# Order of sums, loads and streamed products at the turn from attention to a Strassen-like FFN

## What is computed

```python
h = rmsnorm(x, norm1_gain) * (1.0 + scale1) + shift1
proj = h @ w_in                                   # q | k | v | p
...
x = x + gate1 * (merged @ w_out)
h2 = rmsnorm(x, norm2_gain) * (1.0 + scale2) + shift2
ffn = (silu(h2 @ w_gate) * (h2 @ w_up)) @ w_down
x = x + gate2 * ffn
```

## Time and profile before

| | us |
|---|---|
| median of 3 runs | 1036.49 |
| their lowest and highest | 1035.93, 1039.36 |
| the profiled execution | 1040.24 |
| its span, first to last instruction | 1038.5 |

### The profile page before, as it was taken

How to read it: one execution, slowest core, us unless ns; L and a number is a source line. 1 busy time by engine, 2 the same in 40 slices (tenths; PEclk the granted TensorE clock), 3 DMA queues, 4 the chain that set the end, 5 groups by cost and what they waited for, 6 DMA issues and landing times.

```text
span 1038.5 us, 13419 instructions
## 1 busy us (share of the span) xinstructions
PE 981.9 (95%) x4656; PEld 821.4 (79%) x4656; DVE 695.4 (67%) x1089; ACT 380.8 (37%) x722; POOL 213.2 (21%) x167
## 2 busy tenths in 40 slices
PE   6989999989988798999999999999999999999998
PEld 6878888877876676878788787887878788787876
DVE  4777887885688595765756566565656666665554
ACT  1756667575343453142231413223141322304120
POOL 2032233344221003122220112222011222202220
PEclk9999999999999898999999999999999999999999
DMA  9963333445134365445233543533454253345223
GB/s 363 364 235 132 126 134 120 153 159 192 52 122 142 102 215 210 162 144 213 90 137 145 202 162 121 206 117 122 162 203 162 95 195 130 146 162 201 81 81 162
DMA packets 83669, 166.69 MB, mean 161 GB/s; under 512 B 5312, under 2 KB 52144, under 8 KB 83632
## 3 DMA queue, kind: packets, MB, share of 16 engines
q1 hardware_dynamic: 78400, 155.28, 42.3%
q10 hardware_dynamic: 5232, 10.95, 2.9%
HBM read 151.13 MB, written 15.07 MB: 160 GB/s over the span
## 4 chain that ended last, share of the span: by engine, by line
PE 70%; DMA 11%; DVE 9%; ACT 3%; SPq 3%; issue 2%; POOL 1%; ACTq 1%; DVEq 0%
PE ps L1581 22%; PE ps L1582 22%; PE ps L1583 22%; DMA bs<-bs_scratch 7%; DMA wi_raw<-in_w_in 2%; SPq L416 1%; DVE x L1197 1%; DMA bs_scratch<-stg 1%; DVE wo_raw L1177 1%; PE ps L1692 1%; PE ps L1794 1%; DVE g_acc L1119 1%; SPq L418 1%; DVE xn L1354 1%; DMA sinks<-in_attn_sinks 1%
## 5 line engine op out<-in xcount | busy, mean ns | idle before, releaser
L1437 DVE TENSOR_TENSOR x<-x,ps 128x512 f32<-128x512 f32 x176 | 120.8, 687 | 83.6 <-PE ps L1583 82.8
L1581 PE MATMUL ps<-h_hi,ring 128*128 128x512 f32 x352 | 137.6, 391 | 0.0
L1582 PE MATMUL ps<-h_lo,ring 128*128 128x512 f32 x352 | 137.2, 390 | 0.0
L1583 PE MATMUL ps<-h_hi,ring 128*128 128x512 f32 x352 | 137.2, 390 | 0.0
L1581 PE MATMUL ps<-wd_hi,act_hi 128*128 128x512 f32 x352 | 136.9, 389 | 0.0
L1582 PE MATMUL ps<-wd_lo,act_hi 128*128 128x512 f32 x352 | 136.9, 389 | 0.0
L1583 PE MATMUL ps<-wd_hi,act_lo 128*128 128x512 f32 x352 | 136.9, 389 | 0.0
L1581 PE MATMUL ps<-bs,ring 128*128 128x512 f32 x264 | 105.0, 398 | 15.4 <-DMA bs<-bs_scratch 15.4
L1043 POOL TENSOR_TENSOR wd_lo<-raw_d,wd_hi 128x1024 fp32r<-128x1024 f32 x22 | 57.4, 2628 | 301.0 <-ACT wd_hi L813 301.0
L1393 DVE TENSOR_TENSOR ring<-s,ring 128x512 fp32r<-128x512 f32 x88 | 73.8, 841 | 60.6 <-ACT ring L782 60.4
L1038 POOL TENSOR_TENSOR raw_d<-raw_d,g2bc 128x1024 f32<-128x1024 f32 x22 | 57.3, 2625 | 234.6 <-DMA raw_d<-in_w_down 234.6
(11 more groups left out here) (215 smaller groups left out, 1795.8 us busy)
## 6 DMA issues: line engine op xcount, KB each, us to landing
bs<-bs_scratch SPq DMA_DIRECT2D x126, 512.0 KB, 6.0
stage<-in_w_ada SPq DMA_DIRECT2D x24, 512.0 KB, 5.5
raw_g<-in_w_gate SPq DMA_DIRECT2D x11, 1024.0 KB, 5.1
raw_u<-in_w_up SPq DMA_DIRECT2D x11, 1024.0 KB, 7.1
raw_d<-in_w_down SPq DMA_DIRECT2D x11, 1024.0 KB, 8.9
wi_raw<-in_w_in SPq DMA_DIRECT2D x8, 640.0 KB, 18.8
x_st<-in_x ACTq DMA_DIRECT2D x8, 512.0 KB, 5.3
ada_in_raw<-in_w_ada SPq DMA_DIRECT2D x8, 512.0 KB, 8.5
```

What stands on the lines that cost most here:

```text
L1437: dve.tensor_tensor(xt, xt, bank(DB[j % 4]), ALU.add).then_inc(down_evac, 1)
L1581: pe.matmul(dst, s_hi, m_hi, start=start, stop=False, skip_group_check=onto)
L1582: pe.matmul(dst, s_hi, m_lo, start=False, stop=False, skip_group_check=onto)
L1583: return pe.matmul(dst, s_lo, m_hi, start=False, stop=stop, skip_group_check=onto)
```

## The change

1. The loads of g1bc and g2bc (512 KB each) go from ACT's list at tile 1 to SP's list ahead of the first stage loads.
2. At tile 0 ACT evicts kT before pext.
3. `m_low` of tiles 3 to 7 goes from POOL to DVE.
4. Around tile 7 of stage 2, DVE makes the operands A11 and A12 ahead of the last `t_low` of tile 4, and the sums `a_sum13`, `a_sum2` of pair 0 at other places; ACT's order follows.
5. For tiles 6 and 7 the order of T3, T2, T4, T1, B22 is turned (B22 ahead of T1, T3 behind T2); tile 7's first sum has its own half of g1bc; ACT's wait for `t_back` goes.
6. On SP, the loads of pair 1's raw weights go behind the stores of B22 and the stream load for S4.
7. In every pair A22 is one product (`streamed_products`): gate and up take turns by k.

```diff
-            (6, T3), (6, T2), (7, T2), (7, T3), (6, T4), (7, T4), (6, T1), (7, T1), (6, B22), (7, B22)]
+            (6, T2), (7, T2), (6, T3), (7, T3), (6, T4), (7, T4), (6, B22), (7, B22), (6, T1), (7, T1)]
...
+        def tmp3(t):
+            return g1bc[:, HALF:] if t == 7 else g1bc[:, 0:HALF]
...
-            load_raw(1, 0)
-            load_raw(1, 1)
             store_stage(6, B22)
             store_stage(7, B22)
             sp.wait_ge(t_out, 32 * 4)
             sp.wait_ge(stg_out[0], 32 * 4)
             sp.wait_ge(stg_out[1], 32 * 4)
             load_stream(0, 2, first=True)
+            load_raw(1, 0)
+            load_raw(1, 1)
...
+                    if a == 0:
+                        evac_k(a)
                     act.wait_ge(pT_done, a + 1)
...
-            act.wait_ge(t_back, 16 * 3)
-            t_high(6, T3)
             copy_p1(0, 0, first=True)
...
-                if t + 3 < NT:
-                    m_low(t + 3)
...
             mixed_sum(0, 1)
+            dve.wait_ge(mlo_done, 3)
+            m_low(3)
...
+                    if t == NT - 3:
+                        a_low(0, A11, 0, 0)
+                        a_low(0, A11, 1, 0)
+                        a_low(0, A12, 0, 0)
+                        a_low(0, A12, 1, 0)
+                    t_low(t - 1, B22)
...
+            def streamed_products(p, o, par, dst, n, direct=None):
+
+                for m in range(2):
+                    pe.wait_ge(a_lo, prod(p, o, m))
+                if not direct:
+                    pe.wait_ge(bs_in, 64 * (3 * p + n - 1))
+                for k in range(KT // 2):
+                    b_hi, b_lo = (bs2[0][:, k, :], bs2[1][:, k, :]) if direct == T4 else (bs[:, k, 0, :], bs[:, k, 1, :])
+                    for m in range(2):
+                        r = ring[m][(par + o) % 2]
+                        last = mm3(bank(dst[m]), r[:, 0, k, :], r[:, 1, k, :], b_hi, b_lo, False, k == KT // 2 - 1, True)
+                        if k == KT // 2 - 1:
+                            last.then_inc(prod_done, 1)
+                        elif m == 1 and direct != T4:
+                            last.then_inc(bs_used, 1)
...
-                for m in range(2):
-                    pe.wait_ge(taken, 10 * p + 3 + m)
-                    stream_product(p, A22, m, par, GB, False, 1, T4 if first else None)
+                pe.wait_ge(taken, 10 * p + 4)
+                streamed_products(p, A22, par, GB, 1, T4 if first else None)
```

More of the change, by code:

```diff
@@ L657, in exps, with evac_k @@
                 act.activation(sinkex[:, ch, :], sinkin[:, ch, :], ACT.Exp).then_inc(exp_done, 1)
+            def evac_k(a):
+                act.wait_ge(kT_done, a + 1)
+                kps = bank(6)[:, 0:2 * P].rearrange("p (k c q) -> p k c q", k=NKV, c=2)
+                for ch in range(2):
+                    last = act.activation(kT[:, :, a % 2 + 2 * ch, :], kps[:, :, ch, :], ACT.Copy,
+                                          scale=vcol[:, KG:KG + 1])
+                last.then_inc(kT_evac, 1)
             def evac_ssm(t):
@@ L721, in _ @@
                     evac_o(z, 0)
[L722 to L728, removed]
+                if 1 <= a < NT:
+                    evac_k(a)
                 if it == NT:
@@ L886, in _ @@
             h2_rows_act(7)
+            a_high(0, S2, 1, 0, first=True)
             t_high(6, T2)
-            a_high(0, S2, 1, 0, first=True)
             t_high(7, T2)
+            t_high(6, T3)
             t_high(7, T3)
@@ L897, in _ @@
             a_high(0, A22, 1, 0, first=True)
+            t_high(6, B22)
+            t_high(7, B22)
             t_high(6, T1)
             t_high(7, T1)
-            t_high(6, B22)
-            t_high(7, B22)
             a_high(0, S1, 0, 0, first=True)
@@ L1437, in add_down, with m_low @@
                 dve.tensor_tensor(xt, xt, bank(DB[j % 4]), ALU.add).then_inc(down_evac, 1)
+            def m_low(t):
+                dve.wait_ge(mhi_done, t + 1)
+                dve.tensor_tensor(h_lo[:, :, tok(t)], m_raw[:, :, tok(t)], h_hi[:, :, tok(t)].bitcast(F32),
+                                  ALU.subtract).then_inc(mlo_done, 1)
             mixed_sum(0, 1)
-            for t in range(1, NT):
-                if t + 1 < NT:
-                    mixed_sum(t + 1, 0)
-                if t == NT - 2:
[L1444 to L1448, removed]
-                    a_sum13(0, 0, first=True)
[L1450 to L1467, removed]
@@ new lines, in _ @@
+            dve.wait_ge(mlo_done, 3)
+            m_low(3)
+            for t in range(1, NT - 1):
+                mixed_sum(t + 1, 0)
+                mixed_sum(t, 1)
+                h2_rows(t - 1)
+                if t == NT - 2:
+                    a_sum13(0, 0, first=True)
+                if t - 1 in HALF0:
+                    h2_low(t - 1)
+                    if t + 3 < NT:
+                        m_low(t + 3)
+                else:
+                    t_sums(t - 1)
+                    t_sum4(t - 1)
+                    if t + 3 < NT:
+                        m_low(t + 3)
+                    t_low(t - 1, T3)
+                    t_low(t - 1, T4)
+                    t_low(t - 1, T2)
+                    t_low(t - 1, T1)
+                    if t == NT - 3:
[4 more added lines that the diff above has]
+                    t_low(t - 1, B22)
+                for k in FOLD2.get(t, ()):
+                    fold_gate2(k)
@@ L1468, in _ @@
+            a_sum13(0, 1, first=True)
+            mixed_sum(7, 1)
+            h2_rows(6)
+            a_sum2(0, 0, first=True)
             a_sum2(0, 1, first=True)
-            h2_rows(6)
             t_sums(6)
             t_sum4(6)
-            t_low(6, T3)
             a_low(0, S2, 0, 0)
@@ L1475, in _ @@
             t_sums(7)
+            a_low(0, S2, 1, 0)
             t_low(6, T2)
-            a_low(0, S2, 1, 0)
             t_low(7, T2)
+            t_low(6, T3)
             t_low(7, T3)
@@ L1490, in _ @@
             a_low(0, A22, 1, 0)
+            t_low(6, B22)
+            t_low(7, B22)
             a_sum4(0, 0)
             a_sum4(0, 1)
+            take_sum(u3s, p1s, 0, GB, 0, S3)
             t_low(6, T1)
             t_low(7, T1)
-            take_sum(u3s, p1s, 0, GB, 0, S3)
-            t_low(6, B22)
-            t_low(7, B22)
             take_sum(u3s, p1s, 1, GB, 0, S3)
@@ L1858, in stream_product @@
                 for k in range(KT // 2):
[L1859 to L1862, removed]
+                    last = mm3(bank(dst[m]), r[:, 0, k, :], r[:, 1, k, :], bs[:, k, 0, :], bs[:, k, 1, :],
+                               False, k == KT // 2 - 1, True)
+                    if m == 1 and k < KT // 2 - 1:
                         last.then_inc(bs_used, 1)
@@ L1896, in products_b @@
                     pe.wait_ge(taken, 10 * p + 1 + m)
-                    stream_product(p, S3, m, par, GB, False, 0, T3 if first else None)
+                    stream_product(p, S3, m, par, GB, 0, T3 if first else None)
             def products_c(p, par, first=False):
```

17 lines of the change are left out of this document (8 added, 9 removed).

## The result

The changed kernel takes 1020.69 us (median of 4 runs, 1019.79 to 1021.35) where the kernel before took 1037.92 us in the same measurement (4 runs, 1035.93 to 1040.7): a ratio of 0.983, 95% interval 0.980 to 0.986. It is faster, by 17.2 us or 1.7%. The forecast was 27.2 us of gain, 1009.3 us with a range of 1000 to 1020: too much by 10 us, and the time lies 0.7 us above the range. The profiled execution took 1021.35 us with a span of 1019.6 us, 18.9 us less than the span of before.

What follows compares the result with a forecast made beforehand. PE, busy 981.9 us, was taken as the bound, so only its idle time and slow stretches could be won: 12.6 (term 1) + 13.0 (terms 2 to 5) + 1.6 (term 6) = 27.2, giving 1009.3 us, range 1000 to 1020.

Steps and rivals of the forecast that it cites:

- Term 1: In every pair, A22 by k removes PE's wait for bs ahead of S4: 12.6 us over ten pairs.
- Term 2: Low rests of tiles 3 to 7 from POOL to DVE: DVE reaches tile 7's first sum 2.4 us earlier.
- Term 3: Around tile 7, operands out of PE's way: with Term 2, the awaited x sum ends at 330.9, 7.0 us earlier.
- Term 4: The turn of tiles 6 and 7: B22 is ready at 358.4 us, 19.0 us earlier.
- term 6: The start, at tile 0: issues and pext off the chain, 1.6 us less, bounds -1.0 and +3.3.
- Term 5: Stores and loads between B22 and pair 0's S4: 6.0 us given back, S4 at 380.5, stall some 8 us.
- A: Before pair 0's S4, raw weights do not hold it: S4 starts at 372, time 1001; chance 0.12.
- C: In the pairs, the last slot still lands behind S1: Term 1 gives 0, time 1022; chance 0.07.
- D: In the pairs, coupled halves delay S4's operand: slower than before, 1044 at 3.5 us wait per pair; chance 0.02.
- E: In the pairs, alternating banks costs clock: 2.6 us in each of ten, 1035, no change; chance 0.04.
- B: The turn gives little: terms 2 to 5 give 4 us instead of 13, time 1018; chance 0.12.

Runs made afterwards that it cites:

- the two kernels alone: A22 by k as the only change to the kernel before: 1025.34 us; A22 as two products again on the changed kernel: 1033.56 us.
- mlow_pool: Changed kernel with the low rests of tiles 3 to 7 made by POOL again: 1023.56 us.
- tback: Changed kernel with ACT's wait for the three loads back (t_back) again ahead of pair 0's first copy: 1025.70 us.
- no_turn: Changed kernel with T1 of tiles 6 and 7 made ahead of B22 again, on ACT and DVE: 1025.83 us.
- take_first: Changed kernel with DVE's take of S1's first bank, in pair 0 alone, right behind the takes of A22: 1016.04 us.
- gate2_late: Changed kernel with take_gate2, DVE's copy of the second gate row, moved behind DVE's second half of pair 0: 1023.16 us.
- raws_first: Changed kernel with SP's raw loads of pair 1's gate and up weights ahead of B22's stores again: 1010.99 us.
- sums_late: Changed kernel with DVE's sums of pair 1's weights moved behind the second half of pair 0: 1014.22 us.

## Why the predicted time was too low, step by step

- **Term 1** was right: 12.6 forecast, 12.4 and 12.9 measured by the two kernels alone. In the profiled executions the stretch from S4's end in pair 0 to the end is 11.2 us shorter (636.97 to 625.82): the period came out at 60.06 and not 59.9 us, for the first matmul of S4, which was to lose the 0.27 us above its share, still takes 0.49 us though it waits for nothing.
- **Terms 2 and 3** were right as a position. The second x sum of tile 6 ended at 329.61 us where 330.9 less the start's 1.6 was forecast, and PE's longest wait for x fell from 4.8 to 1.0 us. Term 2 undone costs 2.9 us (mlow_pool), where 2.4 was forecast. Term 3, the place of the eight instructions, was not undone by itself; what it gives in time is not shown.
- **Term 4** was right as a position: the last low rest of B22 ended at 357.26 us (forecast 358.4, 356.8 with term 6). Two parts of it undone, ACT's wait (tback) and the last step of the turn (no_turn), cost 5.0 and 5.1 us. DVE:

```profile
355.97 1.29 DVE L1391 TENSOR_TENSOR stg<-xn,stg 128x512 fp32r<-128x512 f32 x2
```

- **Term 5 is the step that failed**, and within it the sentence "2 sums, 2 of `take_gate2`, a take and a low rest, 6 x 0.6 = 3.8. S4 starts at 380.5". Its transfers were right: the streams went out at 362.36 (363.4 forecast) and raw_u was in at 375.9 (376.7); PE was ready at 372.1 (372). From there S4 took 10.9 us and not 3.8 (6 x 0.6 is 3.6; the sum has a slip of 0.2). I followed S4's operand and forgot its bank: behind the operand DVE does five more instructions and then, as the sixth, the take that frees the bank, some 3.6 us at 0.6 each (take_first: 4.7 us less with that take alone moved). And I set every DVE instruction at 0.6 us, though `take_gate2` sets POOL's scaling free, which then held two others, the low rest of S4's operand and the gate's product behind it, for 3.2 us together (gate2_late: S4 4.4 us sooner without the scaling and the 1.2 us of the copy). So the stall was 14.7 us in place of 8, S4 started 7.9 us later than the forecast with its start term, and with the 1.4 us by which the pairs gave less than term 1 and an S4 that ran 1.0 us shorter, this is the 8.3 us between 27.2 and the 18.9 of the profiled executions.
- The price that the prediction gave to the moved raw loads was too low with it. It put the time that is given back between B22's last low rest and S4 at 6.0 us; that stretch went from 16.1 us (377.39 to 393.46) to 29.5 (357.26 to 386.78), 13.4 us more, and raws_first shows 9.7 us for the moved loads with what hangs on them. A margin on S4's start would have held the result: the range had bounds for rivals that moved the time down to 1000, and none for a later gate.
- **Term 6** cannot be told from none in time; the wait that it was to shorten did shorten, from 2.2 to 0.5 us.

The undone edits together are 12.9 + 2.9 + 5.0 + 5.1 + 1.1 = 27.0 us, and the raw loads' move takes 9.7 back: 17.3, where 17.2 was measured. That match is luck in part: each number has an error of some 3 us, and term 3 and the rest of the turn are not among them. It doesn't rule out a further cause of a few us. What is shown is the stall: sums_late took it away, and take_first, raws_first and gate2_late moved its parts one by one.

Of the rivals, A had the right place and the wrong sign: the raw loads did not land before DVE wanted them. C and D are excluded by term 1's kernels and by the pairs' period, E by the clock of 1.00 in the pairs. B needs a closer look. Its amount came nearly true: all edits but term 1 give some 4.5 us and not 13.0 + 1.6, and its 1018 lies nearer to 1020.7 than 1009.3 does. Its causes did not: the turn's last step carries over (no_turn), and PE has no wait for the read-back of T3 left. The gain was lost behind the turn, at S4.

The Trainium skill, in "DMA: Bandwidth & Descriptors", section "Anatomy of one DMA — SWDGE (gpsimd) path", gives its formula for a single transfer issued from GpSimd, while these were six issued from SP. By the estimate worked out from it, the 4 MB would be in 11.6 us after the first issue; the trace has 13.5 (362.36 to 375.9), near the 13.3 that the prediction took from rows.

## What to carry to other kernels

A matmul group that adds onto a bank has two gates, its operands and the bank; follow both through the other engine's list before you price a stall. When a load is moved to relieve a queue, look at who waits for it in program order: work for the next stage that stands ahead of work for this one turns any slack of that load into a stall. Where a stall is moved and not removed, its new size needs a range of its own.

## What the runs showed of the hardware

**POOL holds DVE, but not every instruction of it.** While POOL worked on two operands in SBUF (378.49 to 383.59), DVE's instructions with all operands in SBUF took 2.48 and 2.12 us and the one that reads PSUM 0.68 (rows above). This was left open in term 2. The Trainium skill, in "SBUF — State Buffer", section "SBUF: two separate sides", has DVE and POOL lock a shared pair of ports for a whole instruction, and counts a DVE instruction among those that need the pair when it has two inputs in SBUF; the trace agrees, since the take has only one.

**Slow stretches come and go between executions.** The changed kernel and take_first have the same program up to 359 us. Both leave PE idle for most of 80 to 82 us; only one has the slow stretch behind it. Windows of after, then of take_first (PEclk is the third number from the end):

```profile
80.00:82.00 2.00, 0.13 (x2) 0.00 (x0) 1.90 (x2) 1.91 (x5) 0.00 (x0) 1.00 0.66 229
82.00:86.00 4.00, 3.88 (x16) 3.38 (x17) 2.74 (x3) 3.00 (x6) 1.00 (x2) 0.57 0.84 287
```

```profile
80.00:82.00 2.00, 0.38 (x4) 0.41 (x5) 1.79 (x3) 1.96 (x4) 0.00 (x0) 1.00 0.63 174
82.00:86.00 4.00, 4.00 (x30) 3.74 (x29) 2.34 (x2) 3.63 (x9) 1.49 (x3) 1.00 0.88 308
```

PE did 16 matmuls in one and 30 in the other. DVE's sum into s_sb starts 0.5 us later in the changed kernel ahead of this stretch (68.24 against 67.75 us) and 2.2 us later behind it (93.15 against 90.97). Stretches of this sort moved the streams' issue between 359.6 and 364.9 us in kernels that have the same program up to there (gate2_late has another one from 300 to 330 us, granted clock 0.94 where the changed kernel has 1.00). Why they come in one execution and not in another is not shown. So two profiled executions are best compared from a common event onwards, and not by their spans.
